# Down products of 96-wide experts on column quarters, and 24 modulation columns moved to the second mixer

## What is computed

```python
for l in range(DEPTH):                      # first block
    ada = cs @ ada_w[l] + ada_b[l]          # 6 x 1024 values: shift, scale, gate of mixer and FFN
    h = rmsnorm(x, norm_mix_g[l]) * (1.0 + sc1) + sh1
    x = x + g1 * token_mixer(h, l, ...)
    h = rmsnorm(x, norm_ffn_g[l]) * (1.0 + sc2) + sh2
    f = swiglu(h, ffn_w1, ffn_w3, ffn_w2) if l == 0 else moe_swiglu(h, ...)
    x = x + g2 * f

def moe_swiglu(h, router, w1, w3, w2):      # comb: weights of the top 2 of 8 experts, else 0
    for e in range(N_EXPERTS):
        out = out + comb[:, e:e + 1] * ((silu(t @ w1[e]) * (t @ w3[e])) @ w2[e])
```

## Time and profile before

| | us |
|---|---|
| median of 3 runs | 2861.55 |
| lowest and highest of them | 2857.86, 2862.45 |
| profiled execution | 2865.6 |
| its span (first to last instruction) | 2863.9 |
| TensorE busy | 2793.9 (98%) |
| VectorE busy | 945.7 (33%) |
| ScalarE busy | 530.1 (19%) |

### The profile page before, as it was taken

One profiled execution on the slowest core, in us unless ns is written; L12 is line 12 of the kernel. 1 busy time (PEld: TensorE's weight loads), 2 busy tenths in 40 slices (PEclk: granted clock), 3 DMA queues, 4 the chain that ended last, 5 costly groups with the idle time before them and its releaser, 6 DMA issues.

```text
span 2863.9 us, 42555 instructions
## 1 busy us (share of the span) xinstructions
PE 2793.9 (98%) x17857; PEld 2137.5 (75%) x17857; DVE 945.7 (33%) x2191; ACT 530.1 (19%) x1104; POOL 94.1 (3%) x181
## 2 busy tenths in 40 slices
PE   7999999899999999999999999999999998999999
PEld 6789988778888655445536537778998896889888
DVE  2654443354411011101101104554355226643330
ACT  3332000233210001001101103243121023331110
POOL 0000111000000000000000000000011000000000
PEclk9999999999989999999999999999999999999999
DMA  8535786533289979998998994332377542323432
GB/s 367 196 127 222 298 305 259 207 118 125 96 339 426 425 299 426 425 415 352 425 428 344 425 409 165 116 118 100 140 254 257 220 171 111 118 107 141 179 118 96
DMA packets 71468, 706.44 MB, mean 247 GB/s; under 512 B 7920, under 2 KB 8176, under 8 KB 31728
## 3 DMA queue, kind: packets, MB, share of 16 engines
q1 hardware_dynamic: 45792, 610.92, 52.7%
q0 software_dynamic: 25488, 92.81, 9.0%
HBM read 702.65 MB, written 1.05 MB: 246 GB/s over the span
## 4 chain that ended last, share of the span: by engine, by line
PE 67%; DMA 2%; DVE 2%; ACT 1%; issue 0%; DVEq 0%; ACTq 0%; SPq 0%
PE psum L969 28%; PE psum L1210 7%; PE psum L1222 6%; PE psum L1270 5%; PE psum L1267 4%; PE psum L984 4%; PE psum L1193 4%; PE psum L1273 2%; DMA ring<-in_m 2%; PE psum L1168 1%; PE psum L1033 1%; PE psum L1231 1%; PE psum L1285 1%; PE psum L1119 1%; PE psum L993 1%; PE psum L1083 1%
## 5 line engine op out<-in xcount | busy, mean ns | idle before, releaser
L969 PE MATMUL psum<-hT,ring 128*128 128x256 f32 x4544 | 994.6, 380 | 0.0
L969 PEld LDWEIGHTS psum<-hT,ring 128*128 128x128 f32 x4544 | 859.9, 190 | 122.2 <-ACT work L1526 3.3
L969 PE MATMUL psum<-work,ring 128*128 128x256 f32 x1624 | 353.4, 379 | 0.0
L969 PEld LDWEIGHTS psum<-work,ring 128*128 128x128 f32 x1624 | 308.1, 190 | 42.5 <-ACT work L1395 0.7
L2197 DVE CUSTOM_DVE_ANT_0 mod_in<-mod_in,c_rows,cols 128x1024 f32<-128x1024 f32 x128 | 161.0, 1279 | 64.5 <-DMA mod_in<-in_mods 64.4
L1210 PE MATMUL psum<-ring,work 128*32 128x256 f32 x2688 | 179.2, 380 | 1.4 <-DVE work L2161 0.7
L984 PE MATMUL psum<-hT,ring 128*128 128x128 f32 x1408 | 163.3, 277 | 2.3 <-ACT hT L1471 1.2
L2161 DVE TENSOR_TENSOR work<-work,psum 128x128 f32<-128x128 f32 x119 | 34.2, 287 | 395.0 <-ACT work L1565 387.5
L984 PEld LDWEIGHTS psum<-hT,ring 128*128 128x128 f32 x1408 | 161.5, 194 | 2.9 <-DVE hT L1825 1.3
L1222 PE MATMUL psum<-ring,work 128*64 128x256 f32 x1216 | 139.6, 382 | 0.0
L2318 POOL DMA_DIRECT2D mod_in<-in_mods x152 | 80.7, 531 | 1776.2 <-DVE ada L2197 1685.8
(11 more groups left out here) (248 smaller groups left out, 2585.9 us busy)
## 6 DMA issues: line engine op xcount, KB each, us to landing
ring<-in_m SPq DMA_DIRECT2D x76, 2048.0 KB, 17.6
ring<-in_w_in SPq DMA_DIRECT2D x46, 2048.0 KB, 7.9
mod_in<-in_mods POOLq DMA_DIRECT2D x176, 512.0 KB, 6.0
ring<-in_m SPq DMA_DIRECT2D x42, 1792.0 KB, 17.4
work<-in_m SPq DMA_DIRECT2D x36, 2048.0 KB, 17.9
ring<-in_up SPq DMA_DIRECT2D x22, 2048.0 KB, 7.7
work<-in_m SPq DMA_DIRECT2D x22, 1792.0 KB, 17.4
ring<-in_f SPq DMA_DIRECT2D x11, 2048.0 KB, 8.8
```

The lines of the kernel that those rows point to most:

```text
L969: last = mm(gbank(it["bank"])[:, j, :], wt[:, k, col0 + j * P:col0 + (j + 1) * P], rhs[:, k0 + k, :], start=(n == 0), stop=(n == total - 1))
```

## The change

The output columns of a down block are no longer halved. The w2 matrix is laid out in 7 blocks of 4 k tiles by all 1024 columns (2 MB each), so a pair loads 42 blocks and not 44, with the same bytes in all. In pairs 1 to 3 the wide expert's products become twelve per k tile, 32 wide by 256 columns: three parts (PSUM banks) of four products on the column quarters of the array. Quarter j < 3 of part p holds tokens 32j to 32j+31 for output columns 256p to 256p+255, quarter 3 of part p holds tokens 32p to 32p+31 for the last 256 columns. ScalarE puts them together again with two copies a part. In pair 0 the wide products stay as they are but for the order. The narrow expert now writes to banks 2 and 4 of the second group (sbank), which gather uses too; hence new waits on r_half in gather, and one on the last narrow hid copy (r_hid) before the first narrow block. In the plan, the 24 columns of layer 2 leave the first feed-forward part (36 items stay among its up units, four behind down unit 0 and four behind down unit 1) and go to the mixer of layer 1, which now has 36 items spread over units 2 to 29.

```diff
-        rest = adas(0, 16, 40) if l == 0 else adas(1, 36, 48)
-        at = (3, 4, 4, 5, 6, 6, 7, 8, 10, 12, 14, 16) + tuple(range(18, 30)) if l == 0 else tuple(range(18, 30))
+        if l == 0:
+            rest = adas(0, 16, 40)
+            at = (3, 4, 4, 5, 6, 6, 7, 8, 10, 12, 14, 16) + tuple(range(18, 30))
+        else:
+            rest = adas(1, 36, 48) + adas(2, 0, EARLY_MODS)
+            at = [2 + 28 * j // len(rest) for j in range(len(rest))]
...
-            plan.extend(spread(items, adas(0, 40, 48) + adas(1, 0, 28) + adas(2, 0, 12)))
+            plan.extend(spread(items, adas(0, 40, 48) + adas(1, 0, 28)))
...
-            slots = {0: adas(1, 28, 36) + adas(2, 12, 14), 1: adas(2, 14, EARLY_MODS)}
+            slots = {0: adas(1, 28, 32), 1: adas(1, 32, 36)}
...
                     for half in range(2):
                         o = sbank(3 * n + half)
+                        if q and n and half:
+                            pe.wait_ge(scalar_round, r.at("r_half", q - 1, 1))
...
                 for n in range(2):
                     if q:
+                        pe.wait_ge(scalar_round, r.at("r_half", q - 1, 0))
                         pe.wait_ge(vector_round, r.at("r_weigh", q, n))
...
             def down(r, q):
-                for half in range(2):
-                    banks = [bank_at[q, "down_" + kind, half] for kind in "wn"]
...
-                    for kg in range(4):
-                        for n in range(2):
...
-                            for k in range(7):
...
-                                elif q:
-                                    last = mm(outs[0][0:96, :], hid_flat[:, 96 * f:96 * f + 96], wt[:, k, :],
-                                              start=(f == 0), stop=(f == 27))
...
+                banks = [bank_at[q, "down_w", part] for part in range(3 if q else 2)]
+                outs = [bank_of(r, b) for b in banks]
+
+                def wide(f, wt):
+                    if q == 0:
+                        for half in range(2):
+                            last = mm(outs[half], hid_e[0][:, f, :], wt[:, half * 512:(half + 1) * 512],
+                                      start=(f == 0), stop=(f == 27))
+                        return last
+                    for part in range(3):
+                        for j in range(4):
+                            tokens, cut = (j, part) if j < 3 else (part, 3)
+                            last = mm(outs[part][32 * j:32 * j + 32, 0:T],
+                                      hid_flat[:, 96 * f + 32 * tokens:96 * f + 32 * tokens + 32],
+                                      wt[:, cut * T:(cut + 1) * T], start=(f == 0), stop=(f == 27))
+                    return last
+
+                for kg in range(DOWN_K):
+                    for n in range(2):
...
+                        if n == 0:
+                            for k in range(4):
+                                last = wide(4 * kg + k, wt[:, k, :])
+                        else:
+                            for k in (0, 2):
+                                for half in range(2):
+                                    for j in range(2):
+                                        f = 4 * kg + k + j
+                                        last = mm(sbank(2 + 2 * half)[64 * j:64 * j + 64, :], hid_e[1][:, f, :],
+                                                  wt[:, k + j, half * 512:(half + 1) * 512],
+                                                  start=(f < 2), stop=(f >= 26))
+                        last.then_inc(tensor_round, r.step(("r_down", q, n), ("r_used", g)))
...
+                act.wait_ge(tensor_round, r.at("r_down", q, 0))
+                for part in range(3 if q else 2):
+                    b = bank_at[q, "down_w", part]
+                    o = psum[:, b % GBANKS, :]
+                    if q:
+                        A(y_e[0][32 * part:32 * part + 32, 3 * T:4 * T], o[96:128, 0:T], ACT.Copy).then_inc(
+                            scalar_round, r.step())
+                        last = A(y_e[0][0:96, part * T:(part + 1) * T], o[0:96, 0:T], ACT.Copy)
+                    else:
+                        last = A(y_e[0][:, part * 512:(part + 1) * 512], o, ACT.Copy)
+                    last.then_inc(scalar_round, r.step(("r_evac", b)))
+                act.wait_ge(tensor_round, r.at("r_down", q, 1))
                 for half in range(2):
...
+                    A(y_e[1][:, half * 512:(half + 1) * 512], sbank(2 + 2 * half), ACT.Copy).then_inc(
+                        scalar_round, r.step(("r_half", q, half)))
```

More of the change, by code:

```diff
@@ L29 @@
 FE_U = D_FE // 256
+DOWN_K = D_FE // 512
 EXPERTS = 8
-EXPERT_CHUNKS = FE_U + 8
+EXPERT_CHUNKS = FE_U + DOWN_K
 THIRDS = 3 * FE_U // 2
@@ L645, in bank_numbers @@
             put(q, kind, i)
-        for half in range(2):
-            for kind in "wn":
-                put(q, "down_" + kind, half)
+        for part in range(3 if q else 2):
+            put(q, "down_w", part)
         for kind in "wn":
@@ L903, in _ @@
                                 else:
-                                    at = c - FE_U
-                                    src, width = arrays["m2"][expert[n], at // 4, at % 4], 7 * 512
+                                    src, width = arrays["m2"][expert[n], c - FE_U], SLOT
                                 if g >= ROUND_RING:
@@ new lines, in down @@
+                for kg in range(DOWN_K):
+                    for n in range(2):
+                        g = q * PAIR_CHUNKS + 2 * (FE_U + kg) + n
+                        wt = block(r, g).rearrange("p (k n) -> p k n", n=D)
+                        to = 4 * kg + 4
+                        if n:
+                            if kg == 0:
+                                pe.wait_ge(vector_round, r.at("r_back", q))
+                            pe.wait_ge(scalar_round, r.at("r_hid", q, "n", (to - 1) // 2 if kg else FE_U - 1))
+                        elif q:
+                            pe.wait_ge(scalar_round, r.at("r_hid", q, "w", (3 * to - 1) // 4))
+                        else:
+                            pe.wait_ge(vector_round, r.at("r_evac", bank_at[q, "w", (to - 1) // 2]))
+                        if n == 0:
[10 more added lines that the diff above has]
+                        last.then_inc(tensor_round, r.step(("r_down", q, n), ("r_used", g)))
@@ L1282, in scatter @@
                         o = bank_of(r, b)
-                        pe.wait_ge(scalar_round, r.at("r_evac", bank_at[q, "down_" + "wn"[n], u // 2]))
+                        if n:
+                            pe.wait_ge(scalar_round, r.at("r_half", q, u // 2))
+                        else:
+                            pe.wait_ge(scalar_round, r.at("r_evac", bank_at[q, "down_w", min(u, 2) if q else u // 2]))
                         for j in range(2):
@@ L2378, in lay_out @@
     a["m13"] = np.stack([pairs(w1, w3, P) for w1, w3 in zip(i["moe_w1"][0], i["moe_w3"][0])])
-    a["m2"] = i["moe_w2"][0].reshape(EXPERTS, 4, 7, P, 2, 512).transpose(0, 4, 1, 3, 2, 5).reshape(EXPERTS, 2, 4, P, -1)
+    a["m2"] = i["moe_w2"][0].reshape(EXPERTS, DOWN_K, 4, P, D).transpose(0, 1, 3, 2, 4).reshape(EXPERTS, DOWN_K, P, -1)
     w = i["w_in_2"]
```

20 lines of the change are left out of this document (removed).

## The result

The changed kernel takes 2815.68 us (median, 2813.78 to 2817.07) where the kernel before took 2860.38 beside it: 44.7 us less, a ratio of 0.9845 with a 95% interval of 0.9829 to 0.986. The forecast was 52.4 us less, 2809.2 us. The sign and the range (2802 to 2816) held, the range by 0.3 us; the centre was 6.5 us too low. The profiled execution took 2813.78 us, with a span of 2812.1.

The account below looks back on a forecast made before the run. TensorE bounds the kernel, with the DMA's weight loads close behind in the experts. Gains of 3.6 (pair 0), 32.7 (three downs) and 16.1 us (columns) sum to 52.4 us, forecasting 2809.2 us from the median, range 2802 to 2816.

Parts of the forecast that it names:

- The columns: After the first FFN: moving 24 modulation columns to layer 1's mixer removes TensorE's wait, 16.1 us gained, bounds 14.1 and 17.
- rival (c): Layer 1's mixer: VectorE is late there with the added columns, by 16 us, giving 2825 us; chance 0.08.
- Pair 0: Pair 0's down keeps its 128-wide products and falls from 78.2 to 74.6 us, 3.6 us gained in full.
- The group of four: Wide down products, pairs 1 to 3: four quarter products take 0.449 us, as in the up thirds; bounds 0.442 and 0.56.
- (b): Wide down products: groups cost 0.56 us, so a pair saves 6.0 us, giving 2823.9 us; chance 0.06.
- (d): Wide down products: quarters overlap only in twos, 48 us more, 2910 us; slower from 0.70 us a group; chance 0.04.
- The DMA's pace: Downs of pairs 1 to 3: weight loads bind at 9.80 us a block pair, saving 10.9 us a pair, not 15.3.
- (a): Downs of pairs 1 to 3: the DMA doesn't bind because the ring hides it, 65.6 us gained, 2796.0 us; chance 0.06.
- Nothing before that is changed.: Pair 2: up to the first narrow down block's landing at 1428.9 us and the up's end, timing stays as before.
- 11 x 4.90: Pair 2's down: the last wide block lands eleven blocks of 4.90 us after the first narrow one, at 1482.8 us.
- The waits and the pause.: Downs of pairs 1 to 3: TensorE waits about 0.8 us a block pair; the DMA's 11 us pause at gather vanishes.
- Copies and waits: ScalarE's output copies and the new waits in gather and down cost 0 us, bounds 0 and 2.

Follow-up runs that it names:

- the columns alone: The kernel before with only the plan of the modulation columns changed, down products and blocks as before: 2843.05 us, ratio 0.9942.
- the half loads: The changed kernel with each down block loading only its first half, 1 MB and not 2, TensorE's work the same: 2794.37 us (one run).
- the 96x512 form: The changed kernel with half the narrow down products left out and wide products of pairs 1 to 3 as 96 wide by 512 columns: 2799.89 us.

## Why the prediction was right, and where it missed

**The columns** (16.1 us): 16.10 in the traces, 16.8 in the medians of the columns alone. What was late next was named rightly: nothing, as in the earlier trace rows. That 24 more columns in layer 1's mixer cost nothing held too: TensorE has no gap there from 525 to 750 us. The margin was thin: with twelve more it waits 5.9 to 7.4 us there, the wait of rival (c).

**Pair 0** (3.6): 3.7; its down takes 74.47 us, forecast 74.6.

**The group of four** (0.449 us): 5.36 to 5.43 us for twelve, 0.447 to 0.452. Rivals (b) and (d) fall with it (by its own sum (d)'s break-even is 0.71 us a group, not 0.70). Where TensorE runs free, twelve take 5.32 us, 0.443, the lower bound. The Trainium skill's 3.07 times ("TensorE: Matmul & The Clock Gate", Measured speedup vs the span model) stands there for four row tiles (K = 32, N = 512), not for column tiles with K = 128; the prediction carried it over. It doesn't hold for this form: if a 32-wide product alone takes what a full-width one of 256 columns does, 0.4415 us, four of them in 0.443 are 3.98 times.

**The DMA's pace** (10.9 a pair): the mechanism was right, and (a) is what the half loads made of the kernel, 2794.4 us for its 2796.0. The size was off: 8.0 to 8.6, so 2.3 to 2.9 us a pair and 8.0 in all, which is the whole difference between 52.4 and 44.5. A down takes 69.3, 69.8 and 69.7 us, not 67.2. Two steps failed, which together make 2.2 to 2.6 us a pair:

- "Nothing before that is changed." The first two down blocks, which land before the point from which I counted, are themselves 2 MB now and were 1.75. The first narrow one lands 5.3 us after the up's end (1396.36), not 4.2 as 1428.9 had it. With both at their old size a pair is 1.0 to 1.2 us shorter.
- "11 x 4.90." The clean spacing is 4.89, but the eleven landings take 54.9 to 55.4 us, not 53.9. Before, where the same bytes came with 2 instruction packets a down and not 6, all fourteen later spacings lay within 0.06 us of 4.29, and this is where I read the pace. Against the 96x512 form the quarters bring 1.2 to 1.4 us of late landings; that their fetched code is the cause is argued, as said above.

**The waits and the pause.** TensorE waits 6.8 us in pair 2's down, 1.0 a block pair where I said 0.8. The seventh block lands 8.5 and 9.5 us behind the sixth at pairs 2 and 3, where it was 19.2 and 17.5. Against 4.9 a pause of some 4 us remains at that place, no longer one of 11; the prediction had none. The ups take 151.0 us (1273.69 to 1424.73) before and 151.3 (1239.80 to 1391.08) after, so that step held. The two windows after, in a down and behind it:

```profile
1400.00:1460.00 60.00, 53.28 (x672) 24.58 (x672) 0.00 (x0) 2.27 (x6) 0.00 (x0) 1.00 1.01 426
```

```profile
1239.80:1261.00 21.20, 21.20 (x192) 17.53 (x194) 7.87 (x19) 3.75 (x7) 0.00 (x0) 1.00 0.99 417
```

The 426 GB/s stand beside the 428 of the earlier trace rows. The Trainium skill gives 358 GB/s as what binds loads from HBM ("DMA: Bandwidth & Descriptors", Where 436 GB/s comes from), but calls its own measured 425 GB/s for 16 MB near the fabric's rate in the same place. The trace agrees with the 425; the 358 don't bind the one core here.

**Copies and waits** (0): the gather takes 7.34 us as before, with no wait inside.

**The base.** I took 4.05 us off for the profiled execution being slower than the median. That fits, since the 3.9 us by which it was behind the one after lay at the start, where the change does nothing.

**Luck.** That the range held is luck in part. It gave the DMA's pace 1 us a pair, and the downs missed by 8.0 us in all; the allowances for the columns, the copies and the runs' spread, which weren't needed, took that up. And the base helped: from the median of 2861.55 us that I started from, 44.7 us less would have been 2816.9 us, outside the range.

## What to carry to other kernels

When an edit takes a stage from TensorE's pace to the DMA's, follow the loads from the last one whose issue the ring holds back to the last one that is waited for, and count every byte between, those of other queues and of the first blocks of the new size too; what TensorE saves beyond that is lost. Here 3.15 MB of small loads on another queue, seemingly free while TensorE bound, were worth 7 us a pair once it didn't. And a stretch that hides 36 small jobs without a trace may not hide 48: here 7.4 us of waits came back.

## What the runs showed of the hardware

- Four 32-wide products on the four column quarters overlap: 96 records (48 products) of 256 columns take 5.32 us, 0.443 us a group. That is the time of one full-width product of 256 columns (16 of them in 7.07 us).
- Code may not be free for the loads. Twelve products a k tile for two brought 5 more instruction packets of 16 KB into a down and 1.2 to 1.4 us of late landings, in a stretch in which the DMA was busy throughout; that the packets are the cause is argued, and one down had six of them with 0.1 us.
- A wait for VectorE can cost more than its idle time. These are windows of the kernel with twelve more columns in layer 0's mixer, around its first wait (granted clock, DMA share and GB/s at the end of each row):

```profile
225.00:230.00 5.00, 5.00 (x25) 4.41 (x24) 2.58 (x4) 4.97 (x4) 1.06 (x2) 1.00 0.99 333
230.00:235.00 5.00, 0.85 (x4) 0.40 (x3) 1.06 (x1) 0.91 (x1) 0.00 (x0) 0.83 0.96 402
235.00:240.00 5.00, 4.11 (x10) 3.27 (x11) 4.54 (x9) 0.00 (x0) 1.58 (x3) 0.50 0.71 222
240.00:245.00 5.00, 5.00 (x25) 4.41 (x24) 3.48 (x6) 0.00 (x0) 1.05 (x2) 0.99 0.78 274
```

  TensorE was idle for 5.04 us and came back at half its clock, 1.2 GHz: 10 records in 4.11 us, where the next 5 us hold 25. That is some 2.1 us beyond the 5.04. Behind the second wait, 5.77 us, 32 records took 10.23 us and not 7.07. The wait of 3.07 us in the kernel with 60 columns in the first FFN cost hardly more than itself: the clock stayed whole, and the 160 records behind it took 34.80 us (34.70 for the same number elsewhere).
